# Causal score widths in one attention, and three-pass fp32r products in another, of a two-block transformer forward

## What is computed

```python
H, dk = DA_HEADS, DA_HEAD_DIM                     # 8, 64
q, k, v = jnp.split(x @ w_qkv, 3, axis=-1)        # q, k: (B, S, H, 2, dk); rope on q and k
def block(args):                                  # two blocks of 128 queries
    qblk, i = args
    s = jnp.einsum('bqhcd,bkhcd->bhcqk', qblk, k).astype(jnp.float32) * scale
    mask = kpos[None, :] <= qpos[:, None]
    s = jnp.where(mask, s, jnp.finfo(jnp.float32).min)
    p = jax.nn.softmax(s, axis=-1)
    a = p[:, :, 0] - lam * p[:, :, 1]
    return jnp.einsum('bhqk,bkhe->bqhe', a.astype(v.dtype), v)
```

```python
def project(h):
    u = h @ w_in                                  # 1024 -> 1024 (q) + 256 (k) + 256 (v)
q_c, k_c, v_c = project(h_ctx)
q_l, k_l, v_l = project(h_lat)
q_l, k_l = apply_rope(q_l, cos, sin), apply_rope(k_l, cos, sin)
s_ctx = jnp.einsum('bqgrd,bkgd->bgrqk', q_b, k_c).astype(F32) * scale
s_loc = jnp.where(m_b, jnp.einsum('bqgrd,bkgd->bgrqk', q_b, k_b) * scale, NEG_INF)
p = sink_softmax(jnp.concatenate([s_ctx, s_loc], axis=-1), sink)
y_lat = o_l.reshape(B, L, SW_HQ * SW_HD) @ w_out
```

## Time and profile before

| | |
|---|---|
| runs | 2772.57, 2773.66, 2777.3 us; median 2773.66 |
| profiled execution | 2774.7 us, of it 2772.6 the span of the trace |
| PE | 2532.5 us busy, 91% of the span; weight loads 60% |
| DVE | 1457.2 us, 53% |
| ACT | 459.8 us, 17% |
| POOL | 62.5 us, 2% |
| DMA | 709.11 MB in all |
| chain that ended last | PE 59%, DMA 23%, issue 11%, DVE 5% |

### The profile page before, as it was taken

One profiled execution on the slowest core, in us unless ns is written; L12 is line 12 of the kernel. 1 busy time (PEld: TensorE's weight loads), 2 busy tenths in 40 slices (PEclk: granted clock), 3 DMA queues, 4 the chain that ended last, 5 costly groups with the idle time before them and its releaser, 6 DMA issues.

```text
span 2772.6 us, 36456 instructions
## 1 busy us (share of the span) xinstructions
PE 2532.5 (91%) x14310; PEld 1676.7 (60%) x14310; DVE 1457.2 (53%) x2407; ACT 459.8 (17%) x893; POOL 62.5 (2%) x108
## 2 busy tenths in 40 slices
PE   7999999999999989998999879999998997778776
PEld 7997777999899579974555433333333763233333
DVE  6767554876876568764777732323225443112113
ACT  0003424100100130001111011111110532111111
POOL 1000000000000000000000000000000000000000
PEclk9999999999999999998999989999998998888888
DMA  7567642555556654573112579999997418999997
GB/s 251 190 222 270 225 145 91 179 182 197 167 183 217 253 193 151 190 265 105 61 61 106 188 309 422 422 422 422 422 421 302 183 68 329 421 422 422 422 422 305
DMA packets 233311, 709.11 MB, mean 256 GB/s; under 512 B 12581, under 2 KB 134453, under 8 KB 177792
## 3 DMA queue, kind: packets, MB, share of 16 engines
q1 hardware_dynamic: 223328, 676.37, 63.3%
q0 software_dynamic: 9312, 30.06, 3.2%
q10 hardware_dynamic: 576, 1.35, 0.2%
HBM read 706.59 MB, written 1.15 MB: 255 GB/s over the span
## 4 chain that ended last, share of the span: by engine, by line
PE 59%; DMA 23%; issue 11%; DVE 5%; ACT 1%; SPq 0%; POOL 0%; ACTq 0%; DVEq 0%; POOLq 0%
PE work L829 43%; DMA ring<-in_moe_up 14%; PE acc L829 14%; DMA ring<-in_moe_down 7%; PE work L845 2%; DMA ring<-in_ffn_w_in 1%; DMA ring<-in_ada_w 1%; SPq L689 0%; DVE stats L2208 0%; DVE rows_h L2225 0%; DVE ring_parts L2068 0%; DVE stats L2174 0%; DVE rows_x L2187 0%; DVE rows_x L2168 0%; DMA rows_x<-in_x 0%
## 5 line engine op out<-in xcount | busy, mean ns | idle before, releaser
L829 PE MATMUL work<-ring,scratch 128*64 128x512 f32 (+1 forms) x3008 | 556.8, 645 | 101.5 <-DMA ring<-in_moe_up 63.8
L829 PE MATMUL work<-rows_h_parts,ring_parts 128*128 128x256 f32 x3072 | 551.2, 286 | 19.4 <-DVE ring_parts L2061 8.3
L829 PEld LDWEIGHTS work<-rows_h_parts,ring_parts 128*128 128x128 f32 x3072 | 478.1, 195 | 23.7 <-issue 9.9
L829 PEld LDWEIGHTS work<-ring,scratch 128*64 128x64 f32 (+1 forms) x3008 | 146.5, 127 | 488.2 <-issue 285.2
L829 PE MATMUL work<-cols_x_parts,ring_parts 128*128 128x256 f32 x1536 | 415.3, 286 | 0.0
L2061 DVE TENSOR_TENSOR ring_parts<-ring,ring_parts 128x2048 fp32r<-128x2048 f32 x132 | 302.6, 2292 | 4.5
L829 PEld LDWEIGHTS work<-cols_x_parts,ring_parts 128*128 128x128 f32 x1536 | 288.0, 195 | 1.6
L829 PE MATMUL acc<-ring_parts,rows_h_parts 128*128 128x512 f32 x896 | 264.3, 391 | 0.0
L829 PE MATMUL work<-cols_x,ring 128*128 128x512 f32 (+1 forms) x640 | 226.2, 513 | 3.9 <-DVE ring L2452 2.9
L2610 DVE COPY scratch<-work 128x512 f32<-128x512 f32 x32 | 22.1, 692 | 368.6 <-PE work L829 368.6
L829 PE MATMUL work<-scratch 128*128 128x256 f32 (+4 forms) x1040 | 199.2, 379 | 6.5 <-issue 4.2
(11 more groups left out here) (273 smaller groups left out, 2584.8 us busy)
## 6 DMA issues: line engine op xcount, KB each, us to landing
ring<-in_moe_down SPq DMA_DIRECT2D x128, 1024.0 KB, 25.6
ring<-in_moe_up SPq DMA_DIRECT2D x127, 1024.0 KB, 26.3
ring<-in_moe_gate SPq DMA_DIRECT2D x121, 1024.0 KB, 24.9
ring<-in_ffn_w_in SPq DMA_DIRECT2D x88, 1024.0 KB, 6.6
ring<-in_ada_w SPq DMA_DIRECT2D x48, 1024.0 KB, 9.8
ring<-in_ffn_w_out SPq DMA_DIRECT2D x44, 1024.0 KB, 6.8
ring<-in_xa_wkv SPq DMA_DIRECT2D x16, 1024.0 KB, 6.7
ring<-in_da_w_qkv SPq DMA_DIRECT2D x12, 1024.0 KB, 6.6
```

The source lines that it names most:

```text
L829: ins = nc.tensor.matmul(o, lhsT, rhs, start=start, stop=stop, **kw)
```

## The change

It has two parts. In the first attention `da_scores`, the maximum, the exponentials and the weighing work only on the columns that a block of queries can see: 128 keys for block 0, 256 for block 1; and the mask is added on the block's own 128 columns only. Transposes and outputs stay.

In the second attention the query, the key and value, and the output products are made in three fp32r passes instead of one float32 product. The high parts of their ten weight pieces are made by ScalarE, the low parts by GpSimd (`weight_low`, the first use of GpSimd for that); the low parts of the columns by VectorE, the high parts of the context's columns by ScalarE. Each of the loads takes two slots of the ring instead of one.

```diff
-               "xa_norm1")
+               "xa_norm1", "mod_norm1", "sw_cols")
...
-    plan.add("sw_q", loads=4, tiles=4)
+    plan.add("sw_q", loads=8, splits=4, tiles=4)
     plan.add("ctx_cols", tiles=4)
-    plan.add("sw_kv", loads=2, tiles=4)
+    plan.add("sw_kv", loads=4, splits=2, tiles=4)
...
-    plan.add("sw_out", loads=4, acc=1)
+    plan.add("sw_out", loads=8, splits=4, acc=1)
...
             def da_scores(o, j, h, signal):
 
-                mm(o[:, 0:S], q_lo[:, h, j * P:(j + 1) * P], k_cols[:, h, :], True, False)
-                mm(o[:, 0:S], ident, mask[:, j, :], False, True)
-                mm(o[:, S:2 * S], q_hi[:, h, j * P:(j + 1) * P], k_cols[:, h, :], True, False)
-                mm(o[:, S:2 * S], ident, mask[:, j, :], False, True, signal)
+                w, own = (j + 1) * P, slice(j * P, (j + 1) * P)
+                for c, q in enumerate((q_lo, q_hi)):
+                    mm(o[:, c * S:c * S + w], q[:, h, own], k_cols[:, h, 0:w], True, False)
+                    mm(o[:, c * S + j * P:c * S + w], ident, mask[:, j, own], False, True, signal if c else None)
...
-            normed_to_cols("mod_norm1", rows_h)
+            normed_to_cols("mod_norm1", rows_h, read=False)
             at = plan["sw_q"]
-            rows_out(at.loads, at.tiles, cols_x, 2)
+            rows_out_split("sw_q", (sw_x_high, x_low), "mod_norm1", 2)
...
             for half in range(2):
-                landed(n + half)
-                w = slot(n + half, 4)
-                for q in range(2 * NT):
-                    for k in range(4):
-                        kk = 4 * half + k
-                        mm(outs[q], cols_x[:, kk, q * P:(q + 1) * P], w[:, k, :], kk == 0, kk == KB - 1,
-                           tile_full[(kv + q) % 4] if kk == KB - 1 else None, done=int(q == 2 * NT - 1 and k == 3))
+                weight_high_done(n + 2 * half)
+                ws = parts(n + 2 * half, 4)
+                for part, (q0, wp, xp) in enumerate(((0, 0, 0), (0, 0, 1), (NT, 0, 0), (NT, 0, 1), (0, 1, 0), (NT, 1, 0))):
+                    if wp and not q0:
+                        split_done("sw_kv", half)
+                    elif q0 and not half and not wp:
+                        pe.wait_ge((sw_ctx_high_ready, sw_ctx_low_ready)[xp], 4 if not xp else 1)
...
-            all_read(plan["sw_cols"].tiles)
-            out_product("sw_out")
+            out_product_split("sw_out", "sw_cols")
...
             def da_exps(u, t):
+                w = (u // DA_H + 1) * P
                 for c in range(2):
-                    ins = nc.scalar.activation(probs[:, u % 2, c * S:(c + 1) * S], work[:, t % 4, c * S:(c + 1) * S],
+                    ins = nc.scalar.activation(probs[:, u % 2, c * S:c * S + w], work[:, t % 4, c * S:c * S + w],
...
             norm_root("mod_norm1", 0, 0)
             ada_out(4)
-            norm("mod_norm1", rooted=1)
-
-            for j in range(NT):
-                norm_root("mod_norm1", NT + j, NT + j)
+            weight_high("sw_q", 0)
+            split_cols("mod_norm1", 0, sw_x_high)
+            norm_root("mod_norm1", 1, 1)
+            split_cols("mod_norm1", 1, sw_x_high)
+            weight_high("sw_q", 1)
+            norm_root("mod_norm1", NT, NT)
+            weight_high("sw_q", 2)
+            norm_root("mod_norm1", NT + 1, NT + 1)
+            weight_high("sw_q", 3)
+            for k in range(2):
+                weight_high("sw_kv", k)
             for j in range(NT):
                 cols_from_rows(plan["ctx_cols"].tiles + 2 * j, (NT + j) * P)
+            for q in range(4):
+                read_out(act, plan["ctx_cols"].tiles + q)
+            for half in range(2):
+                nc.scalar.activation(ctx_x_high[half], cols_x[:, 4 * half:4 * half + 4, S:2 * S],
+                                     ACT.Copy).then_inc(sw_ctx_high_ready, 2)
...
             ada_out(5)
+            for k in range(2):
+                weight_high("sw_out", k)
             attention("sw_att", SW_HQ, sw_exps, lambda j: 4, turned_p=sw_turned)
-            rows_to_cols("sw_cols")
+            for j in range(NT):
+                split_tiles(plan["sw_cols"].tiles + 2 * j, j)
+            for k in range(2, 4):
+                weight_high("sw_out", k)
...
-            mod_norm("mod_norm1", [0, 1])
+            def main_low():
+                for j in range(NT):
+                    cols_low(col_tile("mod_norm1", j, 0), j, sw_x_high)
+
+            mod_norm("mod_norm1", [0, 1], between=main_low)
...
+            for half in range(2):
+                dve.wait_ge(sw_ctx_high_ready, 2 * half + 2)
+                k = slice(4 * half, 4 * half + 4)
+                ins = nc.vector.tensor_tensor(ctx_x_low[:, k, :], cols_x[:, k, S:2 * S], ctx_x_high[half].bitcast(F32), ALU.subtract)
...
                 filled(dve, t)
+                if q == 0:
+
+                    for more in range(1, 2 * NT):
+                        filled(dve, t + more)
...
+            def weight_low(stage, k):
+
+                n = plan[stage].loads + 2 * k
+                pool.wait_ge(load_landed[(n + 1) % RING], 16 * ((n + 1) // RING + 1))
+                nc.gpsimd.tensor_tensor(ring_parts[:, n % RING, :], ring[:, n % RING, :],
+                                        ring_parts[:, (n + 1) % RING, :].bitcast(F32), ALU.subtract).then_inc(split_ready, 1)
...
             rows_until(before_ctx + 28)
+            for k in range(4):
+                weight_low("sw_q", k)
+            for k in range(2):
+                weight_low("sw_kv", k)
             store_mods(4)
             store_mods(5)
             rows_until(before_ctx + 32)
+            for k in range(4):
+                weight_low("sw_out", k)
```

More of the change, by code:

```diff
@@ L911, in _, with rows_out_split @@
             SPLIT_ORDER = ((0, 0), (0, 1), (1, 0))
-            def rows_out_split(stage, xs, x_stage):
+            def rows_out_split(stage, xs, x_stage, blocks=6):
                 at = plan[stage]
-                for cb in range(6):
+                for cb in range(blocks):
                     t = at.tiles + NT * cb
@@ L1614, in _, with kv_x @@
             outs = [open_tile(kv + q) for q in range(2 * NT)]
-            for half in range(2):
-                landed(n + half)
-                w = slot(n + half, 4)
-                for q in range(2 * NT):
-                    for k in range(4):
-                        kk = 4 * half + k
-                        mm(outs[q], cols_x[:, kk, q * P:(q + 1) * P], w[:, k, :], kk == 0, kk == KB - 1,
-                           tile_full[(kv + q) % 4] if kk == KB - 1 else None, done=int(q == 2 * NT - 1 and k == 3))
+            def kv_x(q, xp, kk):
+                c = slice(q % NT * P, q % NT * P + P)
+                if q < NT:
+                    return (sw_x_high, x_low)[xp][:, kk, c]
+                return ctx_x_low[:, kk, c] if xp else ctx_x_high[kk // 4][:, kk % 4, c]
+            for half in range(2):
+                weight_high_done(n + 2 * half)
[5 more added lines that the diff above has]
+                        pe.wait_ge((sw_ctx_high_ready, sw_ctx_low_ready)[xp], 4 if not xp else 1)
+                    for q in range(q0, q0 + NT):
+                        for k in range(4):
+                            fin = bool(wp and half and k == 3)
+                            mm(outs[q], kv_x(q, xp, 4 * half + k), ws[wp][:, k, :], not half and not wp and not xp and k == 0, fin,
+                               tile_full[(kv + q) % 4] if fin else None, done=2 * int(bool(wp and q == 2 * NT - 1 and k == 3)))
             t = plan["sw_turn"].tiles
@@ L2196, in tile_root, with mod_norm @@
                 newton_root(spread[:, c], root[:, c], rstd[:, c], newton[:, c])
-            def mod_norm(stage, streams, mix=None, out_bias=False, last=False, dst=lambda i: rows_h[:, i, :]):
+            def mod_norm(stage, streams, mix=None, out_bias=False, last=False, dst=lambda i: rows_h[:, i, :],
+                         between=None):
                 at = plan[stage]
@@ L2231, in mod_norm @@
                 for s in streams:
+                    if s and between is not None:
+                        between()
                     mine = range(NT * s, NT * (s + 1))
@@ L2306, in da_weigh @@
                 step(nc.vector.tensor_tensor(s[:, 1:2], s[:, 1:2], lam[:, 0:1], ALU.mult))
-                first, second = probs[:, u % 2, 0:S], probs[:, u % 2, S:2 * S]
+                w = (u // DA_H + 1) * P
+                first, second = probs[:, u % 2, 0:w], probs[:, u % 2, S:S + w]
                 step(nc.vector.tensor_scalar(first, first, s[:, 0:1], None, ALU.mult))
@@ L2824, in _ @@
                     step.settle()
+            for half in range(2):
+                dve.wait_ge(sw_ctx_high_ready, 2 * half + 2)
+                k = slice(4 * half, 4 * half + 4)
+                ins = nc.vector.tensor_tensor(ctx_x_low[:, k, :], cols_x[:, k, S:2 * S], ctx_x_high[half].bitcast(F32), ALU.subtract)
+                if half:
```

(6 more changed lines are left out.)

12 lines of the change are left out of this document (8 added, 4 removed).

## The result

The changed kernel takes 2787.3 us (median of 5 runs, 2786.6 to 2787.9) against 2774.3 (5 runs): the ratio is 1.0045, 95% interval 1.0034 to 1.0057. That is 13.0 us slower; the forecast was 10.8 us slower, 2784.5 us. The profiled execution's span is 2785.7 us, 13.1 over before.

What follows compares the result with a forecast made beforehand. Compute engines were taken to pace both attentions, with nothing behind swallowing changes. Second attention +17.3 (11.3 - 5.9 + 2.5 + 3.5 + 7.2 - 4.3 + 3.0), less 6.5 for the first, gave +10.8: 2784.5 us, range 2764 to 2794.

Steps and rivals of the forecast that it cites:

- First attention: First attention: units fall to 1.65 us in block 0 and 2.13 in block 1, saving 6.5 us, bounds 4 and 8.
- The exclusion: Second attention: a VectorE operation with two SBUF inputs and a GpSimd operation exclude each other; subtractions put at 4.74 us.
- step 2: Rotation: last two subtractions delay the first tile's closing lines 4.1 and 4.5 us, less 2; product starts +11.3 in all.
- step 6: Second attention's first units: two subtractions each hold up one unit's two-input sum for 4.4 us, +7.2 for both.
- Step 1: Context rows' norm: ScalarE's first high part and GpSimd's subtractions make the context rows 4.7 us later.
- Step 4: After the key and value product: VectorE waits for all four tiles before reading, so transposes and ada5 start +2.5 us later.
- Step 5: Between ada5's copy and the first exponential: ScalarE makes two high parts of the output weight, +3.5 us.
- Products: Second attention: three fp32r passes save 5.9 us in the key and value product, 4.3 in the output product.
- Clock: TensorE in the second attention: two more starts at its lower level after waits, 2 x 1.5 = +3.0 us.
- The rival without exclusion: Second attention: no blocking that counts, steps 2 and 6 become -1.1 and 0, total 2764.9 us; chance 0.19.
- the five other terms of the second attention: Second attention without the clock: +11.3 to the key and value product, then -5.9, +2.5, +3.5 with +7.2, and -4.3.

Runs made afterwards that it cites:

- the part alone: Kernel before with only the first attention's change (visible columns), second attention as before: 2765.3 us, ratio 0.9966.
- The last kernel: Kernel with all low parts on VectorE and memsets later, plus query weight's third low part before the context norm, reading after two tiles: 2759.9 us, ratio 0.9943.
- the kernel with copies: Changed kernel with GpSimd's ten low parts made by one-input copies instead of subtractions, products not right: 2767.2 us, ratio 0.9973.

## Why the prediction was right, and where its terms were off

- **First attention, -6.5:** measured -6.8 in its stage, with units of 1.63 us in block 0 (1.65 said) and 2.13 in block 1 (2.13 said); the part alone stands at -9.4 [-13, -6]. That nothing behind it gives this back is shown.
- **The exclusion** was read from two rows of 1 us; it held at ten times that length. Steps 2 and 6 came out as the waits that were named: the two closing lines of the first rotated tile took 2.8 and 4.3 us more (4.1 and 4.5 said), and the pair in the attention held the sink sum up for 8.8 us (two times 4.4 said, in one piece instead of in two units). That it is the cause is shown three times: a third operation lengthened the sum by 3.8 us, moving one pair took 8.1 us out of its stage besides the 3.3 of ScalarE, and the low parts of the key and value weight on VectorE brought that product forward by 7.0.
- **Step 1, +4.7:** measured +6.4. I let the scale row wait for the subtraction in progress alone, and it waited for the next as well, 8.05 us. That the start of the product came out at +12.1 for +11.3 is in part luck: step 1 had been put 1.7 us too low, and the two lines of step 2 1.5 too high (8.6 for 7.1).
- **Step 4, +2.5:** +3.8. The last kernel, which waits for two tiles only, needs 0.9 more than before. The wait for all four tiles and the place of the low part were changed in one kernel, so their shares of the rest of the gain weren't measured apart.
- **Steps 5 and 6, +10.7:** +12.9 with the clock. Step 5 was +3.3 (+3.5 said): the first exponential starts 12.7 us behind ada(5) instead of 9.5. The other 9.6 are step 6 (+7.2 said) and TensorE's lower level behind the long sum, where the granted clock was 0.51 for 3.5 us.
- **Products, -5.9 and -4.3:** -4.9 and -3.3; the first is -3.2 beside a product before at the full clock, from which the -5.9 had been worked out. Three passes cost what the first block's rows said; the product starts at the lower clock (3.75 us for its first eight matmuls, 1.98 for later ones), and the output product's last low parts are late by 1.85 us.
- **Clock, +3.0:** of the right order, but not quite where it was put. ada(5) took 7.09 us for 7.07 before. The key and value product lost 2.7 us (24.5 for 21.8; in the profile of before it had lost 1.7), and the restart behind the long sum 1.8 (an estimate: 5.05 us from the start at 2197.30 to that at 2202.35, where the same rows at the full clock add to 3.3). The stages' sum is +20.6 against 17.3; each of the five other terms of the second attention was 0.8 to 2.2 us too low, which comes to 6.3, and the clock's 3.0 stood for about half of it.
- The rival without exclusion said 2764.9, and three runs stand at 2763.7 to 2767.2. That doesn't bear it out: the kernel with copies still has the exclusion, only shorter, and the one with all low parts on VectorE has 23 us of work more there.
- Two readings in the prediction were off and changed no term: a tile's rotation has six operations, four of them with one SBUF input (not eight and five), and the reciprocal of the earlier trace rows took 0.16 us.

## What to carry to other kernels

Before work goes to GpSimd because it is idle, look at what VectorE does meanwhile: each of its operations with two SBUF inputs, however small, waits for the GpSimd operation in progress and, in two places of three here, for the one that follows it at once; and TensorE, where it runs dry for that, loses clock on top. VectorE did the same subtraction in 2.29 us instead of 4.6, and six of the ten stood behind the rotation, mostly where it waits anyway. The engine and the place of the same work, with the memsets moved and the wait for two tiles, decided 27 us here. When a run's noise is as large as an edit's effect, measure between two milestones of the trace around the edit.

## What the runs showed of the hardware

- GpSimd on 128x2048: a copy to fp32r 1.90 us, a subtraction of two tensors 4.6, of one tensor from itself 3.61. The copy keeps VectorE's two-input operations out all the same (a sum of 0.15 us lasted 3.95).
- VectorE's waiting operation didn't get in between two or three GpSimd operations that followed each other at once (8.05, 8.95, 12.76 us), but did at one place, between lines of 3.19 and 4.71 us, in every trace that has GpSimd's row of three subtractions there. What decides that wasn't found.
- In five traces the record of VectorE's sum of the sink begins 0.18 to 0.31 us before GpSimd's first operation, and it waits for it all the same. Before, the same sum took 0.15 us beside GpSimd's issuing of DMAs, so that alone isn't what held it; the cause stays open.
- Behind an idle time of TensorE of 6.5 us the granted clock was 0.51 for 3.5 us, which cost about 1.8 us (the estimate above); behind 10.4 us it was 0.52 for 10 us, which cost 3 us more than that.
